# Two feed-forward blocks with their down projections computed by seven products a pair of chunks

## The chip, the cores and the metric

One core of one Trainium2 chip runs the whole kernel in one launch. The metric is the device time of one execution in microseconds (us). The kernel before took 758.54 us (median of 3 runs, 758.26 to 759.86). Two executions that differ by less than about 0.2% (1.5 us) can't be told apart here.

## The reference

The input is 256 tokens of width 1024. Two transformer blocks follow one another, each with one layer. What matters here are the two feed-forwards; around them lie projections, two kinds of attention and norms, which the change leaves as they are.

```
first block:   h = rms_norm(x, g);  x = x + (silu(h @ w_gate) * (h @ w_up)) @ w_down      # w_down is 2816 x 1024
second block:  h = rms_norm(x, g);  m = (relu(h @ w_up_2) ** 2) @ w_down_2                # w_down_2 is 4096 x 1024
               x = x + rms_norm(m, g_post)
```

Everything is in 32-bit floats. The kernel reaches that precision with a rounded 32-bit format on TensorE: a value v is split into `hi` (v rounded) and `lo` (v - hi, rounded), and each product a*b is the sum of three matmuls, hi*hi, hi*lo and lo*hi.

## The kernel before, in words

**Layout.** The 256 tokens are two tiles of 128 rows. Weights come in 232 "fills" of 128 x 1024 floats (512 KB): SyncE loads a fill into one of 4 raw buffers `w_raw`, ScalarE (ACT) rounds it into `w_hi` (`round_to`, line 1284), VectorE (DVE) subtracts to get `w_lo` (`cut_to`, line 1908), TensorE (PE) multiplies. Fill k can only be loaded when fill k - 4 has been cut. All programs are written out by hand, one in-order queue per engine, with semaphores between them; SyncE's queue of loads is in order too.

**Up projections** (`multiply_up`, line 888). The hidden vector is computed transposed: 128 hidden columns (a "chunk") by 256 tokens, 8 chunks of the contraction by 3 matmuls, each with 256 columns moving. In the first block two chunks of gate and two of up make one step (96 matmuls), 11 steps; in the second four chunks make a step (96 matmuls), 8 steps. A fill holds two of the 8 contraction chunks for the four outputs of a step.

**Down projections** (`multiply_down` through `chunk`, line 453; for the last step line 930). A chunk of the hidden vector times 128 rows of the down weight: 2 token tiles, 3 matmuls, 2 halves of 512 output columns, 12 matmuls of 512 columns a chunk. PSUM banks 4 to 7 keep the four quarters of the output (2 token tiles by 2 column halves) through the whole feed-forward; banks 0 to 3 take the up products. PE does the up part of step i and then the down part of step i - 1.

**Between up and down.** First block: DVE multiplies the gate by the row scale (`scale_gate`, line 2387), ACT applies SiLU (line 1613), DVE multiplies by up (`times_up`, line 2393), ACT rounds (line 1608), DVE cuts (line 2377). Second block: ACT applies ReLU (line 1870), GpSimd (POOL) squares (line 2955), ACT squares and rounds (line 1876), DVE cuts.

**Ends.** First block: `add_residual` (line 2371) adds each quarter, scaled by its row's norm, to x; PE then turns x (lines 582, 593), ACT and DVE split it (lines 1302, 1928), and the next projection starts (line 506). The last down step goes quarter by quarter, so three of the four additions run beside matmuls. Second block: ACT squares each quarter with a row sum (line 1703), DVE scales (line 2553), POOL takes the inverse root (line 2785), DVE adds to x (line 2567), SyncE and ACT store.

Of the kernel before, what the change touches and what calls it, by code (L numbers as in the profile page):

```python
# [10 lines left out]
F32R = mybir.dt.float32r  # L11
# [4 lines left out]
P = 128  # L16
D = 1024
# [22 lines left out]
D_FF2 = 4 * D  # L40
MASKED = -1e30
# [52 lines left out]

def laid_out(inputs):
# [17 lines left out]
    arrays["rope1m"] = np.ascontiguousarray(rope[SEQ:])  # L113
    return arrays
# [5 lines left out]
class Weights:  # L120
# [5 lines left out]
    def __init__(self, a):  # L126
# [11 lines left out]
        n = D_FF // 11  # L138
        for i in range(12):
            if i < 11:  # L140
                self.first["up1", i] = len(self.fills)
                for s in range(4):
                    pieces = []
                    for w, name in enumerate(("w_gate", "w_up")):
                        rows = a[name][0][2 * s * P:(2 * s + 2) * P, i * n:(i + 1) * n].rearrange("(c p) n -> p c n", p=P)
                        pieces.append((lambda raw, w=w: raw.rearrange("p (c w n) -> p c w n", c=2, w=2)[:, :, w, :], rows))
                    self.fills.append(pieces)
            if i > 0:
                self.slab(("down1", i - 1), a["w_down"][0][2 * (i - 1) * P:2 * i * P, :], 2, D)
# [15 lines left out]
        for i in range(9):  # L165
            if i < 8:
                self.slab(("up2", i), a["w_up_2"][0][:, i * WIDE:(i + 1) * WIDE], KC, WIDE)
            if i > 0:
                self.slab(("down2", i - 1), a["w_down_2"][0][4 * (i - 1) * P:4 * i * P, :], 4, D)
# [28 lines left out]
    def used(self, name):  # L198

        last = self.first[name] + {"qb": 4, "kb": 4, "vb": 4, "kva": 2, "qa": 4}.get(name, 4)  # L200
        return last if name[0] != "down1" else last - 2
# [18 lines left out]
spread_done spread_copied gate_scaled acted hidden_done hidden_rounded hidden_cut  # L220
# [6 lines left out]
Semaphores = namedtuple("Semaphores", SEMAPHORES + ["w_landed", "x_landed", "turned_landed", "post_landed", "stored"])  # L227


def program(nc, a, out):  # L230
    with ExitStack() as ctx:
# [6 lines left out]
                       stored=[sems[f"stored{t}"] for t in range(TILES)], **sems)  # L238
# [9 lines left out]
def allocate(nc, ctx, T):  # L248
# [67 lines left out]
    T.ffn_rows = sb("ffn_rows", [P, TILES, WIDE])  # L316
    T.f_hi = sb("ffn_hi", [P, 4, SEQ], F32R)
    T.f_lo = sb("ffn_lo", [P, 4, SEQ], F32R)
# [4 lines left out]
    T.pT2 = sb("pT2", [P, 2, NG + 1, P])  # L323
    T.wspT = sb("w_spatial_T", [P, TILES, TILES, GROUPS, P])
    T.bsp = sb("b_spatial", [P, TILES, GROUPS])
    T.qk = {c: sb(f"{c}2_rows", [P, TILES, WIDE]) for c in "qk"}
# [13 lines left out]
    T.spread = T.u_rows[:, 0, 0:SEQ]  # L340
    T.hid_hi, T.hid_lo = (T.f_hi, T.q2T["q"]), (T.f_lo, T.q2T["k"])
# [35 lines left out]
BANKS = {"qb": 0, "kb": 1, "vb": 3, "oa": 5, "ob": 8, "down1": 11, "b": 14, "o1": 17, "down2": 18}  # L377
FFN1_STEPS, FFN2_STEPS = 11, 8
# [7 lines left out]
def squared(place, t, half):  # L386

    return 2 * t + half + 1 if place == 0 else 4 + 2 * half + t + 1
# [5 lines left out]


def up_banks(i):

    return (4, 5, 6, 7) if i == 0 else (0, 1, 2, 3)
# [12 lines left out]
def sync_program(nc, a, out, T, S, W):  # L411
    sp = nc.sync
    rows_out = rows_of(out)
    sp.dma_start(T.w_raw[:, 0:1, 0:WIDE], W.half).then_inc(S.half_landed, 16)
    for k, pieces in enumerate(W.fills):
# [13 lines left out]
        for view, src in pieces:  # L429
            sp.dma_start(view(T.w_raw[:, r, :]), src).then_inc(S.w_landed[r], 16)  # L430
    for t in range(TILES):
# [8 lines left out]
def tensor_program(nc, T, S, W):  # L440
    pe, bank, ident = nc.tensor, T.bank, T.ident

    def w(half, k, c, per):
        n = SLOT // per
        return half[:, k % SLOTS, c * n:(c + 1) * n]
# [424 lines left out]
    def feed_forward(up, down, steps, chunks, ready, taken, cut0, cut_per, spread, rounded, right=None):  # L870
        def multiply_down(i, first):
            for c in range(chunks):
                k = W.first[down, i] + c
                pe.wait_ge(*W.cut(S, k))
                if c % 2 == 0:
                    pe.wait_ge(S.hidden_cut, cut0 + i * cut_per + c // 2 + 1)
                mm = chunk(T.hid_hi[i % 2], T.hid_lo[i % 2], k, 0, 1, c, ((4, 5), (6, 7)), WIDE, first and c == 0, False)
                mm.then_inc(S.w_used, 1)

        def multiply_up(i, s, c, passes):  # L880

            k, kc = W.first[up, i] + s, 2 * s + c
            w_hi, w_lo = w(T.w_hi, k, c, 2), w(T.w_lo, k, c, 2)
            for b in range(4):
                cols, outs = slice(b * P, (b + 1) * P), bank[up_banks(i)[b]][:, 0:SEQ]
                for n, (x, y) in enumerate(((w_hi, T.h_hi), (w_hi, T.h_lo), (w_lo, T.h_hi))):
                    if n in passes:
                        mm = pe.matmul(outs, x[:, cols], y[:, kc, :], start=kc == 0 and n == 0,  # L888
                                       stop=kc == KC - 1 and n == (1 if i == 0 else 2))
            return mm  # L890
# [2087 lines left out]
```

## Time and profile before

| | |
|---|---|
| median of 3 runs | 758.54 us |
| profiled execution, its own time | 758.59 us |
| span of the profiled execution, first to last instruction | 757.3 us |
| PE busy | 98% of the span |
| DVE busy | 60% |
| ACT busy | 49% |
| GpSimd busy | 15% |
| granted TensorE clock, mean | 0.999 |
| matmuls | 4394 |
| HBM read | 128.6 MB, 171 GB/s over the span |

The span is 1.3 us shorter than the execution's own time; the difference is what lies before the first and behind the last instruction. The feed-forward of the first block lies from 130.8 to 322.5 us of the span, that of the second from 570.0 to the end. Busy times count an instruction from its start to its end; matmuls overlap, so the cost of one is read from the distance between starts.

### The profile page before, as it was taken

The page shows a single profiled execution, that of the slowest core. Times are in us where ns is not written, and L with a number is a line of the kernel's source. Part 1 is how long each engine was busy: PE and PEld are TensorE (multiplying, and loading weights), DVE is VectorE, ACT ScalarE, POOL GpSimd, SP SyncE. Part 2 cuts the span into 40 slices and gives each one's busy share as a digit, 9 for nine tenths or more (in the row PEclk, how much of TensorE's full clock was granted, in tenths as well). Part 3 has the DMA queues.
Part 4 walks back from the last instruction along what each step waited for, and adds up shares of the span by engine and source line. Part 5 has one row for each costly group of instructions (what it writes and reads, how often), then busy time and mean ns, then how long its engine had stood idle before and what let it go on. Part 6 is the DMA issues. An engine that isn't in the chain of part 4 may idle for free.

```text
span 757.3 us, 11043 instructions
## 1 busy us (share of the span) xinstructions
PE 739.8 (98%) x4394; PEld 641.1 (85%) x4394; DVE 457.8 (60%) x635; ACT 373.3 (49%) x535; POOL 112.5 (15%) x138
## 2 busy tenths in 40 slices
PE   6999999999999999999999999999999999999996
PEld 5877778999999999888888888888779899998895
DVE  5898695766555555465747555674948754455433
ACT  6666754644444434285443534664338644444431
POOL 2867550100000000001110000000302111001110
PEclk9999999999999999999999999999999999999999
DMA  9642142787665666446536543474535766656511
GB/s 318 207 132 82 58 160 92 229 284 220 189 212 172 195 216 208 133 142 219 169 110 195 194 139 112 123 250 147 178 107 198 260 192 187 206 184 191 180 46 56
DMA packets 70179, 130.46 MB, mean 172 GB/s; under 512 B 5312, under 2 KB 29072, under 8 KB 70128
## 3 DMA queue, kind: packets, MB, share of 16 engines
q1 hardware_dynamic: 68144, 125.00, 52.3%
q0 software_dynamic: 1552, 4.20, 1.7%
q8 instruction: 35, 0.57, 0.3%
q10 hardware_dynamic: 432, 0.56, 0.2%
q14 instruction: 16, 0.13, 0.0%
HBM read 128.62 MB, written 1.05 MB: 171 GB/s over the span
## 4 chain that ended last, share of the span: by engine, by line
PE 93%; DVE 3%; DMA 2%; issue 1%; ACT 1%; SPq 0%; DVEq 0%; ACTq 0%
PE psum L453 41%; PE psum L888 29%; PE psum L506 12%; PE psum L930 2%; DMA w_raw<-in_w_in 2%; PE psum L680 1%; PE psum L601 1%; PE psum L546 1%; PE psum L631 1%; PE psum L1058 1%; PE psum L582 1%; PE psum L652 1%; DVE b_ratio L2154 0%; PE psum L992 0%; PE psum L1020 0%
## 5 line engine op out<-in xcount | busy, mean ns | idle before, releaser
L1908 DVE TENSOR_TENSOR w_lo<-w_raw,w_hi 128x1024 fp32r<-128x1024 f32 x225 | 275.2, 1235 | 158.3 <-ACT w_hi L1284 157.7
L1284 ACT ACTIVATE w_hi<-w_raw 128x1024 fp32r<-128x1024 f32 x231 | 241.2, 1059 | 180.7 <-PE psum L888 78.6
L888 PE MATMUL psum<-h_hi,w_hi 128*128 128x256 f32 x608 | 170.3, 284 | 0.6 <-issue 0.6
L888 PE MATMUL psum<-h_hi,w_lo 128*128 128x256 f32 x608 | 169.5, 283 | 0.0
L888 PE MATMUL psum<-h_lo,w_hi 128*128 128x256 f32 x608 | 161.8, 281 | 0.0
L888 PEld LDWEIGHTS psum<-h_hi,w_hi 128*128 128x128 f32 x608 | 114.7, 189 | 1.7 <-issue 0.7
L888 PEld LDWEIGHTS psum<-h_hi,w_lo 128*128 128x128 f32 x608 | 114.4, 188 | 0.0
L888 PEld LDWEIGHTS psum<-h_lo,w_hi 128*128 128x128 f32 x608 | 111.1, 189 | 0.7
L453 PE MATMUL psum<-w_hi,h_hi 128*128 128x512 f32 (+1 forms) x240 | 94.5, 394 | 0.0
L453 PE MATMUL psum<-w_hi,h_lo 128*128 128x512 f32 (+1 forms) x240 | 93.0, 387 | 0.0
L453 PE MATMUL psum<-w_lo,h_hi 128*128 128x512 f32 (+1 forms) x240 | 92.9, 387 | 0.0
L453 PEld LDWEIGHTS psum<-w_hi,h_lo 128*128 128x128 f32 x240 | 45.1, 188 | 10.1
L453 PEld LDWEIGHTS psum<-w_lo,h_hi 128*128 128x128 f32 x240 | 45.2, 188 | 9.3
L453 PEld LDWEIGHTS psum<-w_hi,h_hi 128*128 128x128 f32 x240 | 45.1, 188 | 9.2
L506 PE MATMUL psum<-w_hi,h_hi 128*128 128x512 f32 x128 | 52.6, 411 | 0.0
L506 PE MATMUL psum<-w_lo,h_hi 128*128 128x512 f32 x128 | 50.4, 394 | 0.0
L506 PE MATMUL psum<-w_hi,h_lo 128*128 128x512 f32 x128 | 46.6, 395 | 0.0
L453 PE MATMUL psum<-w_hi,ffn_hi 128*128 128x512 f32 x120 | 37.9, 397 | 0.0
L453 PE MATMUL psum<-w_lo,ffn_hi 128*128 128x512 f32 x120 | 37.7, 395 | 0.0
L453 PE MATMUL psum<-w_hi,ffn_lo 128*128 128x512 f32 x120 | 37.6, 394 | 0.0
L2955 POOL TENSOR_TENSOR u_rows<-ffn_rows 128x512 f32<-128x512 f32 x16 | 16.9, 1075 | 135.2 <-ACT ffn_rows L1870 135.2
L506 PEld LDWEIGHTS psum<-w_hi,h_hi 128*128 128x128 f32 x128 | 24.1, 188 | 6.3 <-issue 0.6
(303 smaller groups left out, 992.7 us busy)
## 6 DMA issues: line engine op xcount, KB each, us to landing
w_raw<-in_w_in SPq DMA_DIRECT2D x77, 512.0 KB, 4.5
w_raw<-in_w_down SPq DMA_DIRECT2D x54, 512.0 KB, 4.3
w_raw<-in_w_up SPq DMA_DIRECT2D x32, 512.0 KB, 4.4
w_raw<-in_w_gate SPq DMA_DIRECT2D x44, 256.0 KB, 2.9
w_raw<-in_w_up SPq DMA_DIRECT2D x44, 256.0 KB, 3.4
w_raw<-in_w_out SPq DMA_DIRECT2D x16, 512.0 KB, 4.0
w_raw<-in_w_branch_a SPq DMA_DIRECT2D x4, 512.0 KB, 4.6
w_raw<-in_w_branch_b SPq DMA_DIRECT2D x4, 512.0 KB, 4.6
```

The costliest lines, as they stand in the source:

```text
L453: mm = pe.matmul(bank[b][:, 0:width], x[:, kc, t * P:(t + 1) * P], y[:, h * width:(h + 1) * width], start=first and n == 0, stop=last and ...
L506: mm = pe.matmul(out, x[:, kc, t * P:(t + 1) * P], y, start=n == 0 and i == 0, stop=last and i == 2)
L546: mm = pe.matmul(bank[7][0:32 + META, :], T.meta_stack[:, kc, :], y, start=kc == 0 and n == 0, stop=kc == KC - 1 and n == 1)
L582: tr = pe.transpose(bank[b][:, j * SEQ + t * P:j * SEQ + (t + 1) * P], src[:, t, c * P:(c + 1) * P], ident[:])
L601: tr = pe.transpose(bank[b][:, c * SEQ + t * P:c * SEQ + (t + 1) * P], src[:, t, (2 * n + c) * P:(2 * n + c + 1) * P], ident[:])
L631: mm = pe.matmul(bank[b][:, 0:KEYS], x[rows, c, t * P:(t + 1) * P], y[rows, c // 2 if kind == "a" else c, :], start=i == 0, stop=i == 2)
L652: tr = pe.transpose(bank[MAP_BANK][:, c * SEQ + t * P:c * SEQ + (t + 1) * P], T.maps[:, t, h if kind == "a" else 2 * h, c * P:(c + 1) * P] ...
L888: mm = pe.matmul(outs, x[:, cols], y[:, kc, :], start=kc == 0 and n == 0, stop=kc == KC - 1 and n == (1 if i == 0 else 2))
L930: mm = pe.matmul(bank[4 + 2 * t + h][:], x[last][:, c, t * P:(t + 1) * P], y[:, s, cols], start=False, stop=c == chunks - 1 and n == 2)
L1284: act.activation(T.w_hi[:, k % SLOTS, :], T.w_raw[:, k % RAW_SLOTS, :], ACT.Copy).then_inc(S.w_rounded, 1)
L1908: dve.tensor_tensor(T.w_lo[:, k % SLOTS, :], T.w_raw[:, k % RAW_SLOTS, :], T.w_hi[:, k % SLOTS, :], ALU.subtract).then_inc(S.w_cut, 1)
L2955: pool.tensor_tensor(T.u_rows[:, j, :], rows, rows, ALU.mult).then_inc(S.hidden_done, 1)
```

## The change

The two down projections are computed with the Strassen-Winograd scheme. A pair of chunks of the hidden vector (2 x 128 columns) and the two halves of the output make a 2 x 2 block product: A (tokens by hidden, quarters A11, A12, A21, A22) times B (hidden by output). Instead of 8 products of quarters, 7 products of sums of quarters are accumulated, over all pairs but the last of a feed-forward, in seven PSUM banks (0 to 6). After the last such pair the output quarters are formed from the seven sums once. The last pair is done in the plain way, quarter by quarter (8 products). So a pair costs 21 matmuls of 512 columns instead of 24: 10 of 11 pairs in the first block, 15 of 16 in the second.

What else moves with it:

- The four quarters of a pair's down weight are loaded from a new layout into `pair_raw` (three quarters) and, twice, into `pair_t` (the fourth): 768 KB + 512 KB a pair instead of 1 MB. DVE forms four sums of quarters (`add_pair`, `sum_pair`, `sum_pair_rest`); ACT rounds all seven (`round_pair`, three instructions of 1536, 1024 and 1024 columns), DVE cuts all seven (`cut_pair`, the same sizes). Before, two fills of 1024 were rounded and cut.
- DVE forms four sums of the hidden quarters (`sum_hidden`, `_2`, `_3`: 256, 128 and 128 columns); ACT rounds and DVE cuts seven quarters (896 columns) a pair; before four (512).
- The up weights come in a new layout, one fill for all 8 contraction chunks of 128 hidden columns. The first group of a feed-forward needs two fills at once (`up_first`), which were one before. Up fills go round 4 slots instead of 8, the other 4 slots hold every second pair's seven quarters.
- Up products of chunk after chunk all go into bank 7 (`up_two`). ACT copies them out (`take_up`; in the second block `take_hidden` with ReLU) before the next may start. `scale_gate` and `times_up` work on chunks from SBUF (256 columns) instead of two chunks from PSUM (512).
- The squares of the second block are done by ACT alone (`square_hidden`), not by GpSimd and ACT.
- At the end of each feed-forward DVE forms three intermediate sums and the quarters from the product banks; in the first block GpSimd takes two of the additions (`add_x`).
- SyncE's queue has a pair load behind every second or fourth up fill; a pair load waits until the pair two before it has been cut.

```diff
-    def feed_forward(up, down, steps, chunks, ready, taken, cut0, cut_per, spread, rounded, right=None):
+PRODUCT = {1: (1, 0, 2), 2: (3, 2, 0), 3: (7, 1, 1), 4: (2, 6, 6), 5: (5, 3, 5), 6: (6, 5, 3), 7: (4, 4, 4)}
+EARLY, LATE, LAST = (1, 2, 3), (7, 5, 6, 4), (1, 6, 7, 4, 5, 2, 3)
...
+    def down(q, products, first=False, last=False):
+        buf, i = pair_place(q)
+        pe.wait_ge(S.hidden_cut, q + 1)
+        for n_product, p in enumerate(products):
+            x, y, b = PRODUCT[p]
+            pe.wait_ge(S.pair_cut, pair_parts(q) + NEEDS[p])
...
+            for n, (u, v) in enumerate(((x_hi, y_hi), (x_hi, y_lo), (x_lo, y_hi))):
+                mm = pe.matmul(bank[b][:], u, v, start=first and n == 0, stop=last and n == 2)
...
+    for i in range(2, PAIRS1):                      # PE, first block
...
+        down(i - 2, EARLY, first=i == 2)
+        chunk_up1(2 * i)
...
+        down(i - 2, LATE, first=i == 2)
+        chunk_up1(2 * i + 1)
+    down(LAST1 - 1, LAST, last=True)
+    pe.wait_ge(S.up_taken, 2 * PAIRS1)
+    down_quarters(1)
...
+    for i in range(2, PAIRS2):                      # PE, second block
+        if i > 2:
+            pe.wait_ge(S.up_taken, 2 * PAIRS1 + i)
+            up_two(W.first["up2", 2 * i], 7)
...
+        down(FIRST2 + i - 2, EARLY, first=i == 2)
...
+        down(FIRST2 + i - 2, LATE, first=i == 2)
+    down(LAST2 - 1, LAST, last=True)
+    pe.wait_ge(S.up_taken, 2 * PAIRS1 + PAIRS2)
+    down_quarters(2)
...
+        if i < PAIRS2:                              # DVE, second block, iteration i, q = FIRST2 + i - 1
+            add_pair(q)
+            cut_pair(q, 0)
+            sum_pair(q)
+            sum_hidden(q, 2 * PAIRS1 + i)
+            sum_pair_rest(q)
+            sum_hidden_2(q)
+            cut_pair(q, 1)
+            sum_hidden_3(q)
+            cut_pair(q, 2)
+            cut_to(min(f + 2 * i + 6, len(W.fills)))
...
+        cut_hidden(q)
...
+            for part in range(3):                   # ACT, second block, iteration i
+                round_pair(q, part)
+            take_hidden(i)
+            round_to(min(f + 2 * i + 6, len(W.fills)))
+            square_hidden(i)
...
+        round_hidden(q)
...
+    for i in range(1, PAIRS1):                      # DVE, first block
+        sum_hidden(i - 1, 2 * i)
+        add_pair(i - 1)
+        cut_pair(i - 1, 0)
+        sum_hidden_2(i - 1)
+        scale_gate(2 * i)
+        sum_hidden_3(i - 1)
+        cut_fill(f + 4 * i + 4)
+        sum_pair(i - 1)
+        times_up(2 * i)
+        sum_pair_rest(i - 1)
+        cut_fill(f + 4 * i + 5)
+        cut_hidden(i - 1)
+        cut_pair(i - 1, 1)
+        cut_pair(i - 1, 2)
...
+        scale_gate(2 * i + 1)
+        cut_fill(f + 4 * i + 6)
+        times_up(2 * i + 1)
+        cut_fill(f + 4 * i + 7)
```

## Rows read from the trace of the kernel before

**Rows 1.** The page, part 1: busy us, share, instructions.

```profile
PE 739.8 (98%) x4394; PEld 641.1 (85%) x4394; DVE 457.8 (60%) x635; ACT 373.3 (49%) x535; POOL 112.5 (15%) x138
```

**Rows 2.** The page, part 4: the chain that ended last, by engine.

```profile
PE 93%; DVE 3%; DMA 2%; issue 1%; ACT 1%; SPq 0%; DVEq 0%; ACTq 0%
```

**Rows 3.** Windows of one step of each block: length, busy us by engine, clock, DMA.

```profile
207.85:224.98 17.13, 17.13 (x121) 16.03 (x120) 9.33 (x9) 7.41 (x9) 0.55 (x1) 1.00 0.65 207
615.92:638.64 22.72, 22.72 (x145) 20.53 (x144) 10.92 (x10) 10.38 (x12) 2.04 (x2) 1.00 0.62 187
```

**Rows 4.** The chain in order of time, second block: start, us, work.

```profile
604.49 11.39 PE psum L888 x96
615.88 11.21 PE psum L453 x48
627.09 11.52 PE psum L888 x96
```

**Rows 5.** Groups of VectorE instructions by form: busy us, mean ns.

```profile
L2377 DVE TENSOR_TENSOR k2T<-u_rows,q2T 128x512 fp32r<-128x512 f32 x8 | 5.1, 684 | 0.0
L2371 DVE SCALAR_TENSOR_TENSOR x<-psum,row_scale,x 128x512 f32<-128x512 f32 x4 | 3.0, 750 | 4.8 <-PE psum L930 4.8
```

**Rows 6.** VectorE in order of time: start, us (of a merged run), count.

```profile
137.08 4.63 DVE L1908 TENSOR_TENSOR w_lo<-w_raw,w_hi 128x1024 fp32r<-128x1024 f32 x4
157.35 1.23 DVE L1908 TENSOR_TENSOR w_lo<-w_raw,w_hi 128x1024 fp32r<-128x1024 f32 x1 [1.26 <-ACT w_hi L1284]
734.63 0.15 DVE L2756 SCALAR_TENSOR_TENSOR stat<-row_scale 128x2 f32<-128x2 f32 x1
734.82 0.16 DVE L2758 TENSOR_TENSOR row_scale<-row_scale 128x2 f32<-128x2 f32 x1
```

**Rows 7.** ScalarE in order of time.

```profile
145.45 3.89 ACT L1284 ACTIVATE w_hi<-w_raw 128x1024 fp32r<-128x1024 f32 x4
156.26 1.06 ACT L1284 ACTIVATE w_hi<-w_raw 128x1024 fp32r<-128x1024 f32 x1 [1.42 <-DMA w_raw<-in_w_down]
582.95 1.15 ACT L1876 ACTIVATE ffn_hi<-ffn_rows 128x512 fp32r<-128x512 f32 x2
```

**Rows 8.** In order of time, where the first feed-forward starts: VectorE, TensorE.

```profile
133.52 1.22 DVE L1908 TENSOR_TENSOR w_lo<-w_raw,w_hi 128x1024 fp32r<-128x1024 f32 x1
144.26 0.36 PE L888 MATMUL psum<-h_hi,w_hi 128*128 128x256 f32 x1 [0.56 <-issue]
```

**Rows 9.** In order of time, end of the first feed-forward.

```profile
320.58 0.39 PE L930 MATMUL psum<-w_hi,ffn_lo 128*128 128x512 f32 x1
320.81 1.91 PE L582 MATMUL psum<-small,x 128*128 128x128 f32 x16
322.48 0.47 PE L506 MATMUL psum<-w_hi,h_hi 128*128 128x512 f32 x1
```

**Rows 10.** VectorE's cuts of the hidden vector, 575 to 600 us: ns min/median/max.

```profile
L2377 DVE TENSOR_TENSOR ffn_lo<-u_rows,ffn_hi x2: 678/1096/1514, 583.7 to 585.2; 128x512 fp32r<-128x512 f32 x2
```

**Rows 11.** In order of time, start of the second feed-forward: TensorE, VectorE, SyncE.

```profile
570.03 0.36 PE L888 MATMUL psum<-h_hi,w_hi 128*128 128x256 f32 x1
571.86 2.35 DVE L1908 TENSOR_TENSOR w_lo<-w_raw,w_hi 128x1024 fp32r<-128x1024 f32 x2
574.24 2.29 SPq L430 DMA_DIRECT2D w_raw<-in_w_up  x2
```

**Rows 12.** Transfers from 580 to 600 us.

```profile
DMA packets 2022, 5.55 MB, mean 278 GB/s; under 512 B 161, under 2 KB 161, under 8 KB 2019
w_raw<-in_w_up SPq DMA_DIRECT2D x4, 512.0 KB, 5.1
```

**Rows 13.** In order of time, the end of the kernel.

```profile
751.10 0.40 PE L930 MATMUL psum<-w_hi,k2T 128*128 128x512 f32 x1
753.32 1.41 DVE L2567 SCALAR_TENSOR_TENSOR x<-tmp,stat,x 128x512 f32<-128x512 f32 x2
754.76 0.65 ACTq L1887 DMA_DIRECT2D out<-x  x1
```

More of the change, by code:

```diff
@@ L40 @@
 D_FF2 = 4 * D
+PAIRS1, PAIRS2 = D_FF // (2 * P), D_FF2 // (2 * P)
 MASKED = -1e30
@@ L137, in __init__ @@
             self.slab((name, 0), a["w_out"][0][h * WIDE:(h + 1) * WIDE, :], 4, D)
[L138 to L149, printed above, removed]
+        for f in range(2 * PAIRS1):
+            self.first["up1", f] = len(self.fills)
+            for w in range(2):
+                self.fills.append([(lambda raw: raw, a["up1"][f, :, w, :])])
         win2 = a["w_in_2"][0]
@@ L198, in used @@
     def used(self, name):
[L200 to L201 removed]
+        return self.first[name] + {"kva": 2}.get(name, 4)
 SEMAPHORES = """
@@ new lines, in scalar_program @@
+    f = W.first["up2", 0]
+    round_to(f + 8)
+    round_pair(FIRST2, 0)
+    take_hidden(0)
+    take_hidden(1)
+    square_hidden(0)
+    square_hidden(1)
+    for i in range(2, PAIRS2 + 1):
+        q = FIRST2 + i - 1
+        if i == 2:
+            round_pair(FIRST2, 1)
+            round_pair(FIRST2, 2)
+            round_hidden(FIRST2)
+        if i < PAIRS2:
[4 more added lines that the diff above has]
+            square_hidden(i)
+        else:
+            for part in range(2):
+                round_quarters(q, part)
+        round_hidden(q)
@@ L1886, in scalar_program @@
+    copy_first(2)
+    for n, (t, half) in enumerate(((0, 0), (0, 1), (1, 0), (1, 1))):
+        square_last(n, t, half, T.last[t, half])
     act.wait_ge(S.x_posted, 8)
@@ L2395, in vector_program @@
-    f = W.first["up1", 0]
-    for i in range(FFN1_STEPS):
-        last = i == FFN1_STEPS - 1
-        cut_to(f + 8 if i == 0 else f + 6 * i + 9)
-        scale_gate(i)
-        times_up(i)
-        cut_to(f + 9 if i == 0 else f + 6 * i + 10)
-        if not last:
-            cut_to(f + 10 if i == 0 else f + 6 * i + 11)
-        cut_hidden(i, i, 0, T.ffn_rows[:, i % 2, :].rearrange("p (c n) -> p c n", c=2))
-        if not last:
-            cut_to(f + 6 * i + 12)
-    last = W.first["z", 1]
@@ L2416, in vector_program @@
+    dve.wait_ge(S.product_done, 7)
+    dve.wait_ge(S.x_part, 2)
+    step(add_x(bank[1][:], 1, 1))
+    for n, (t, half, b) in enumerate(QUARTER_BANKS[1]):
+        dve.wait_ge(S.quarter_done, n + 1)
+        own()
+        add_x(bank[b][:], t, half).then_inc(S.x_added, 1)
+    cut_pairs("h3", (0, 1), (5, 6), gain(2), T.h_hi, T.h_lo)
+    cut_pairs("h3", (2, 3), (2, 3), gain(2), T.h_hi, T.h_lo)
     r3 = [T.row_scale[:, 2, t:t + 1] for t in range(TILES)]
@@ L2765, in vector_program @@
     post_add(1, 0, HALVES)
+    scale_last(2)
+    end_last(3)
+    scale_last(3)
     post_mean(1, 1)
-    post_scale(1, 1, 1, 7, T.bg[1], scale[1])
     post_add(1, 1, HALVES)
```

631 lines of the change are left out of this document (435 added, 196 removed).

## The prediction

> **What bounds the kernel now.** Read the page's first part, then the chain of waits, then windows. TensorE is busy 98% of the span [rows 1] and holds 93% of the chain that ended last [rows 2]; DVE (60%) and ACT (49%) have room, on average. One step of either feed-forward shows it stage by stage: 17.13 us and 22.72 us in which TensorE never pauses, while DVE works 9.33 and 10.92 us and ACT 7.41 and 10.38 us [rows 3]. So the reader should expect that fewer matmuls shorten the time, until DVE or ACT, which pay for it, come up to TensorE. The chain in order of time gives the price of a matmul: 96 up matmuls take 11.39 and 11.52 us, so 0.119 us each, and 48 down matmuls 11.21 us, so 0.233 us each [rows 4].
>
> **What goes.** The first block loses 10 x 3 = 30 matmuls of 512 columns, 7.0 us, the second 15 x 3 = 45, 10.5 us. The up matmuls are as many as before. That is the whole gain: 17.5 us if TensorE never waits. Beside it the 0.56 us in which TensorE stood after the first step [rows 8] goes: the wait for the spread scale now stands two chunks later.
>
> **DVE's price.** A cut of 512 columns takes 0.684 us [rows 5], one of 1024 columns 1.23 us [rows 6]: 1.06 ns a column and 0.14 us. But four of 1024 in a row take 4.63 us [rows 6], so they start 1.13 us apart: 1.06 ns a column and only 0.05 us. Where an instruction waits for the one just before it, it starts 0.04 us after that one's end (734.63 + 0.15, then 734.82 [rows 6]), some 0.13 us more. ACT's run of four takes 3.89 us [rows 7], 0.95 us apart; two of 512 columns take 1.15 us, 0.5 us apart [rows 7].
>
> *First block, a pair.* TensorE: 21 x 0.233 + 96 x 0.119 = 16.35 us (17.13 before). DVE: 18 instructions, 12160 columns: 12160 x 1.06 ns + 18 x 0.05 = 13.8 us, with few waits on itself, because another instruction stands between. ACT: 11 instructions, 8448 columns, some 8 us. I laid out one pair from the end of an up chunk (0): ACT takes bank 7 by 0.65, before the 9 EARLY matmuls end at 2.1, so the next chunk isn't held; `cut_hidden` ends at 14.4, where TensorE wants it at 16.35. Steady state: bound by TensorE. Cost 0; if DVE needed 19% more, this cover would be gone.
>
> *Second block, a pair.* TensorE: 21 x 0.233 + 48 x 0.119 = 10.6 us (11.36 before). DVE: 12 instructions, 9088 columns: 9.6 + 0.6 = 10.2 us, and two waits on itself (`sum_pair`, `sum_pair_rest`), 10.45. One iteration: `sum_pair_rest` ends at 4.7; ACT then rounds part 2, takes the chunks, rounds two fills, squares and rounds the hidden quarters: 0.95 + 0.5 + 1.9 + 0.5 + 0.94 = 4.8, so 9.55; DVE's last cut starts at 9.6 and ends its iteration at 10.6. Three engines with the same period: no spare anywhere. I take 10.6 for each, so steady state costs nothing, but a late start is never made good.
>
> **The starts and ends.** These eat the gain.
>
> *Start of the first block.* The second group of `up_first` needs the fill whose cut ends at 133.52 + 1.22 [rows 8]: +0.3. The first pair's hidden sums are ready late, since no down matmuls stretch the first four chunks. Chunk 2 ends near 149.9; DVE is through with chunk 1, the pair's sum and first cut only at 152.1, and needs 5.4 more until `cut_hidden` ends at 157.5; TensorE is there at 155.6: +1.9.
>
> *End of the first block.* In the pair before the last, `cut_quarters` (1.67 + 0.6) puts DVE behind: `scale_gate(21)` at 2.4 after the last up chunk, not 0.7; with two fills and the last `times_up` in between, the last hidden cut ends at 6.05, where the 21 LAST matmuls end at 4.9: +1.15. Then DVE has 12 instructions of 512 columns (0.6 to 0.7 each, four of them waiting on the one before) and waits for GpSimd's second addition, before the four quarters can be added. By my count the last addition ends 15.3 after the last up chunk, TensorE at 11.7. Before, the last matmul and the next projection's first lay 320.58 + 0.23 to 322.48 apart, transposes included: 1.7 us [rows 9]. Now 4.4: +2.7. GpSimd beside a two-input DVE instruction can cost more: one cut beside a square took 1514 ns, another 678 [rows 10]; bound 0 to +1.7 for two such, I take 0.
>
> First block: -7.0 - 0.55 + 0.3 + 1.9 + 1.15 + 2.7 = **-1.5 us**.
>
> *Start of the second block.* `up_first` asks for two fills at once. The first of the two DVE cuts that start at 571.86 is the second fill; it ends at 573.1, where TensorE starts at 570.03 now [rows 11]: +3.1, nothing else can run. Then pair 0: before, the two up fills issued at 574.24 [rows 11] landed in 5.1 us [rows 12]. Now 1.28 MB of pair load stand ahead of them in SyncE's queue; at the 278 GB/s that this stretch reached [rows 12] that is 4.6 us, at most. `round_pair` and `add_pair` of pair 0 stand behind both fills on ACT and DVE, so pair 0 is ready near 594.1 and TensorE, with three chunk pairs done, at 590.5: +3.6 (bounds 0.4, the load hidden, and 4.6). Next, `take_hidden(2)` stands behind all of pair 1's rounding: up pair 3 needs bank 7 at 4.9, ACT is done at 6.3: +1.4. The fill behind two pair loads lands 1.2 late, once: +1.2 (0 to 2).
>
> *End of the second block.* The last two whole pairs have no fills (8.9 us for DVE), but TensorE, 1.4 late in phase, still waits +1.0 for pair 14. After that the quarters: DVE's forms, `end_last`, `scale_last`, mean, root, `post_add` run as 17 instructions of 512 columns from 22 us after the hidden cut of pair 12, to 36.7; the last matmul ends at 28.4. So 8.3 + 2.55 for the store; before, the last matmul (751.4) to DVE's last (754.73) is 3.3 [rows 13] and the store the same 2.55. +5.0 (3 to 7).
>
> Second block: -10.5 + 3.1 + 3.6 + 1.4 + 1.2 + 1.0 + 5.0 = **+4.8 us**.
>
> SiLU, gelu and the masks' loads on GpSimd have slack of tens of us; 0. GpSimd's squares gone: 0, they were off the chain, and DVE has no GpSimd beside it in steady state. The squares of x3 stand ahead of two fills of ACT; the fills are wanted 11 us after the projection starts and are there at 6: 0.
>
> **A rule of the skill.** DVE's row says 1.13 us from start to start of 1024 columns where one alone takes 1.23 [rows 6]. The Trainium skill, "VectorE: DVE Perf Modes", section on the trn2 errata, gives a 32-bit two-input instruction (N + 151)/0.96 ns and says many small instructions pay the fixed part each time; its section "The DRAIN you can't avoid" says the next does not start until the pipe is empty, except where it isn't held. By the full rule a pair of the second block would take DVE 9088/0.96 + 12 x 157 ns = 11.35 us; by the exception the 10.2 above. The trace's runs side with the exception.
>
> **Sum.** In the profiled execution's own frame: 758.59 - 1.5 + 4.8 = **761.9 us**; the median of the runs, 758.54, is the same within 0.1.
>
> **Rivals.**
>
> *DVE unhidden (slower still).* If 512- and 128-column instructions with semaphores don't overlap like the runs of 1024, each costs its full 0.14 us and the waits: 9088 x 1.06 + 12 x 0.14 = 11.3 us a pair. For: a DVE that waits for ACT at each step never starts early. Against: the order puts other work between. Twelve pairs with fills at +0.7 to +0.9: +8 to +11, so 771 us.
>
> *Transfers bind (slower).* A pair of the second block moves 2.3 MB in 10.6 us, 222 GB/s, issued in one burst behind the last cut of the pair before. 278 GB/s were reached over 20 us [rows 12]; if bursts with the doubled quarter only reach 200, a pair takes 11.8: +13, 775 us.
>
> *Faster: the waits at the starts aren't there.* The mechanism: SyncE's loads overtake, so that the two fills land in 5.1 us despite the pair load ahead, pair 0 is ready with TensorE (0.4 instead of 3.6), DVE then runs ahead of TensorE by more than the 1.4 of phase, and those 1.4, 1.2 and 1.0 vanish too. -6.8: 755.1 us. It decides from DVE's iteration taking under 10.3 us: then lateness is made good over 12 pairs. For it: transfers share 16 engines and don't queue strictly. Against: ACT's chain of 9.55.
>
> *No change.* Only half of that: the fills land in time, the rest stays, 758.7 us.
>
> **Chances.** Forecast 0.50; DVE unhidden 0.12; transfers bind 0.08; faster 0.15; no change 0.15. A measurement of this kernel tells 0.2%, 1.5 us. So faster 0.15, same 0.15, slower 0.70. The range: below, it reaches to the faster case but not past it, 756; above, to the lower part of the DVE case, 769. Outside lie some 0.2.
>
> **What would show it.** The windows of one step: 16.4 us in the first block and 10.6 us a pair in the second, DVE busy over 95% in the latter. TensorE idle before the first up group of the second block near 3 us, and before its first down matmul 3 to 4 us. After the last matmul 10 to 11 us to the end of the span. If a pair of the second block takes 11.3 or more, DVE's overlap is the failed step; if TensorE doesn't wait for the first pairs, the landing times are. Wrong altogether would be a first block that isn't at 16.4 a pair.

## The result, and the profile after

The changed kernel took 774.08 us (median of 4 runs, 772.60 to 775.98), the kernel before 758.71 in the same session: a ratio of 1.0202, 95% interval 1.0176 to 1.0227. The direction was right, the size was not: 761.9 was forecast and 756 to 769 the range. The profiled execution is the slowest of the four, 775.98 us, 1.9 above the median; its span is 774.7 us.

The page of the kernel after, part 1, the engines of part 4 and one row of part 6, which answer to [rows 1, 2, 12]:

```profile
PE 732.0 (94%) x4319; PEld 631.0 (81%) x4319; DVE 598.0 (77%) x852; ACT 433.2 (56%) x611; POOL 101.8 (13%) x126
...
PE 69%; DVE 16%; DMA 8%; issue 4%; ACT 2%; POOL 1%; SPq 0%; ACTq 0%; DVEq 0%
...
w_raw<-in_up SPq DMA_DIRECT2D x76, 512.0 KB, 5.1
```

There are 75 matmuls fewer, as meant. The chain tells the rest: TensorE held 93% of it and now holds 69%; DVE and the transfers of up fills took the difference. Part 6 hides the latter, because its median is over all fills. So the next view is the chain in order of time, where the second block starts and behind (start, us, work; kernel after):

```profile
578.45 9.77 DMA w_raw<-in_up
588.29 1.07 ACT w_hi L1429
...
599.12 1.04 DVE hidden_lo L2654
...
623.34 9.00 DMA w_raw<-in_up
...
655.24 10.38 DMA w_raw<-in_up
...
677.96 10.73 DMA w_raw<-in_up
...
701.04 9.54 DMA w_raw<-in_up
```

From 578 us to 711 us the chain goes through DVE and, in about every second pair, through an up fill that takes 9 to 11 us from its issue to its landing, where [rows 12] had 5.1.

**Steady pairs.** Windows of the kernel after, as [rows 3] (length, busy us by engine PE, PEld, DVE, ACT, POOL, clock, DMA share, GB/s): one pair of the first block, two of the second, and a longer stretch of the second.

```profile
209.00:225.40 16.40, 16.40 (x121) 15.46 (x120) 14.44 (x19) 9.72 (x12) 0.55 (x1) 1.00 0.72 231
645.44:668.16 22.72, 22.72 (x151) 20.42 (x151) 21.39 (x25) 14.84 (x17) 0.00 (x0) 1.00 0.65 218
650.50:692.70 42.20, 40.72 (x267) 36.48 (x267) 39.09 (x45) 28.50 (x31) 0.00 (x0) 1.00 0.61 207
```

The first block's pair is 16.4 us, as forecast (16.35). In the second block TensorE would do four pairs of 10.55 in the 42.2 us of the third row, and it stands for 1.5 of them. The starts of `hidden_lo` (`cut_hidden`), one a pair, give the period: 599.07, 612.85, 623.41, 634.88, 645.44, 656.29, 668.16, 678.72, 691.24, 701.80, 713.12, 723.89, 734.45. The first period is 13.8 us; of the eleven behind it five are 10.56 us and six lie between 10.8 and 12.5. These eleven take 121.6 us, where 11 x 10.55 is 116.05.

**Where the time lies.** Starts of the first matmul of each stage, profiled executions:

| stage | before | after | longer | forecast |
|---|---|---|---|---|
| start to first up matmul | 130.79 | 131.77 | +0.98 | 0 |
| first feed-forward, to the next projection's first matmul | 191.69 | 194.42 | +2.73 | -1.5 |
| from there to the second feed-forward's first matmul | 247.55 | 250.97 | +3.42 | +3.1 |
| second feed-forward, to the end of the span | 187.27 | 197.54 | +10.27 | +1.7 |
| span | 757.3 | 774.7 | +17.4 | +3.3 |

(The forecast's +4.8 for the second block contains the 3.1 of the third line.) Two lines hold the miss: 4.2 us in the first feed-forward, 8.6 in the second. The +0.98 of the first line isn't the change's: the kernels of experiments 1 to 4 have the same instructions up to there and start at 130.30 to 130.54.

TensorE's waits, kernel after: before the first down matmul of the first block, its second instruction (at half the clock: the third starts at 160.81, 0.43 us behind it, where [rows 4] had 0.233), before the last pair's quarters, the transposes; second block: first up matmul, first down matmul, the down's second half.

```profile
159.82 0.76 PE L1024 MATMUL psum<-pair_hi,hidden_hi 128*128 128x512 f32 x1 [3.39 <-issue]
160.38 0.63 PE L1024 MATMUL psum<-pair_lo,hidden_hi 128*128 128x512 f32 x1
...
315.16 0.47 PE L1044 MATMUL psum<-pair_hi,hidden_hi 128*128 128x512 f32 x1 [1.43 <-issue]
...
323.80 2.63 PE L684 MATMUL psum<-small,x 128*128 128x128 f32 x16 [2.93 <-DVE x L2715]
...
577.16 0.55 PE L978 MATMUL psum<-h_hi,w_hi 128*128 128x256 f32 x1 [2.98 <-ACT h_hi L1444]
...
600.26 0.76 PE L1024 MATMUL psum<-pair_hi,hidden_hi 128*128 128x512 f32 x1 [3.64 <-issue]
...
606.38 0.80 PE L1024 MATMUL psum<-pair_hi,hidden_hi 128*128 128x512 f32 x1 [1.95 <-ACT up_rows L2073]
...
763.48 0.40 PE L1044 MATMUL psum<-w_hi,hidden_lo 128*128 128x512 f32 x1
```

The releaser of the fifth row is misnamed, as can happen with a wait for several: the first quarter of `h_hi`, which is all that this matmul needs of it, was there before 574.3; what ended at 577.07 is DVE's cut of the second fill. Experiment 1 moves that cut alone, and the wait is gone. Windows behind three of these waits, kernel after (granted clock is the third from the end):

```profile
159.82:164.00 4.18, 4.18 (x10) 3.31 (x11) 4.18 (x6) 2.09 (x4) 0.00 (x0) 0.50 0.57 211
577.16:582.22 5.06, 5.06 (x24) 5.06 (x25) 5.06 (x9) 3.25 (x4) 1.17 (x1) 0.53 0.69 194
600.26:609.40 9.14, 7.19 (x16) 5.20 (x17) 7.10 (x9) 3.02 (x5) 0.00 (x0) 0.51 0.79 275
```

Before, the clock was 1.00 at these places. A granted clock of 0.50 is the lower level, 1.2 GHz: after each of these three stretches without work TensorE ran at half speed, for about 5.7, 4.8 and 9.0 us, the last with the wait of 1.95 us in it. After the 2.93 us before the transposes it did not: there the clock is 1.00 (313.7 to 327 us). In the profiled executions of experiments 1, 2 and 4, which have the same instructions there, it did fall (0.65, 0.62 and 0.76 over the transposes). So the lower clock doesn't follow each such wait. How much of the time it is, experiments 4 to 6 measure.

### The profile page after: what moved, and what is told of

Same layout as the page of the kernel before. It is cut to its first block, busy times and chain, and to the rows that moved or that the text cites. A ratio compares the mean times of both kernels' runs of the same rounds, so it can differ in the third digit from the quotient of the medians.

```text
span 774.7 us, 11228 instructions
## 1 busy us (share of the span) xinstructions
PE 732.0 (94%) x4319; PEld 631.0 (81%) x4319; DVE 598.0 (77%) x852; ACT 433.2 (56%) x611; POOL 101.8 (13%) x126
## 4 chain that ended last, share of the span: by engine, by line
PE 69%; DVE 16%; DMA 8%; issue 4%; ACT 2%; POOL 1%; SPq 0%; ACTq 0%; DVEq 0%
PE psum L555 22%; PE psum L978 17%; PE psum L608 12%; PE psum L1024 8%; DMA w_raw<-in_up 6%; DVE w_lo L2138 3%; DVE w_lo L2603 2%; DMA w_raw<-in_w_in 2%; DVE pair_lo L2603 2%; PE psum L782 1%; DVE pair_sums L2616 1%; DVE hidden_lo L2654 1%; PE psum L703 1%; PE psum L648 1%; PE psum L733 1%
## 5 line engine op out<-in xcount | busy, mean ns | idle before, releaser
L2138 DVE TENSOR_TENSOR w_lo<-w_raw,w_hi 128x1024 fp32r<-128x1024 f32 x171 | 209.5, 1239 | 48.3 <-ACT w_hi L1429 47.8
L1429 ACT ACTIVATE w_hi<-w_raw 128x1024 fp32r<-128x1024 f32 x177 | 184.1, 1058 | 61.3 <-DMA w_raw<-in_w_in 36.0
L978 PE MATMUL psum<-h_lo,w_hi 128*128 128x256 f32 x608 | 164.2, 283 | 0.0
L978 PEld LDWEIGHTS psum<-h_hi,w_hi 128*128 128x128 f32 x608 | 116.0, 191 | 10.2 <-ACT up_rows L2073 5.5
L978 PEld LDWEIGHTS psum<-h_hi,w_lo 128*128 128x128 f32 x608 | 116.0, 191 | 0.0
L555 PEld LDWEIGHTS psum<-w_hi,h_hi 128*128 128x128 f32 x240 | 45.1, 188 | 9.2
L1801 ACT ACTIVATE up_rows<-psum 128x512 f32<-128x512 f32 x22 | 13.1, 597 | 65.5 <-PE psum L978 65.5
L1024 PE MATMUL psum<-pair_hi,hidden_hi 128*128 128x512 f32 x91 | 38.3, 420 | 9.9 <-issue 7.0
L1768 ACT ACTIVATE pair_hi<-pair_raw 128x1536 fp32r<-128x1536 f32 (+1 forms) x26 | 32.9, 1265 | 18.3 <-DVE pair_raw L2629 18.3
L1768 ACT ACTIVATE w_hi<-tmp 128x1536 fp32r<-128x1536 f32 (+1 forms) x24 | 30.4, 1265 | 16.8 <-DVE tmp L2629 16.8
L2603 DVE TENSOR_TENSOR pair_lo<-pair_raw,pair_hi 128x1536 fp32r<-128x1536 f32 (+1 forms) x26 | 38.6, 1486 | 0.0
```

The source lines that it names most:

```text
L555: mm = pe.matmul(bank[b][:, 0:width], x[:, kc, t * P:(t + 1) * P], y[:, h * width:(h + 1) * width], start=first and n == 0, stop=last and ...
L978: mm = pe.matmul(out, x, y[:, kc, :], start=kc == 0 and n == 0, stop=kc == KC - 1 and n == last_pass)
L1024: mm = pe.matmul(bank[b][:], u, v, start=first and n == 0, stop=last and n == 2)
L1429: act.activation(T.w_hi[:, W.slot[k], :], T.w_raw[:, k % RAW_SLOTS, :], ACT.Copy).then_inc(S.w_rounded, 1)
L1768: act.activation(T.pair_hi[buf][:, places, :], src, ACT.Copy).then_inc(S.pair_rounded, 1)
L1801: act.activation(T.rows[:, j % 2, :].rearrange("p (c n) -> p c n", c=2), src, ACT.Copy).then_inc(S.up_taken, 1)
```

## The experiments

Theory at the start: the 12 us that my sum missed are not in the steady pairs' work but in three starts: (a) waits at the beginning of each block, (b) the half clock behind them, (c) pair loads ahead of up fills in SyncE's queue. The rival: the scheme as such is too expensive for DVE, whatever the order.

**1. The second up fill earlier.** DVE cuts it before the input's halves.

```diff
+    cut_fill(W.first["up2", 0] + 1)
     post_out(1)
     add_out2(1)
     cut_h4(0)
     cut_h4(1)
-    cut_fill(W.first["up2", 0] + 1)
     cut_fill(W.first["up2", 0] + 2)
```

> The changed kernel (774.1 us), with VectorE's cut of the second up fill of the second block moved ahead of the post-norm of the second token tile, into a stretch where VectorE has 1.5 us to spare. The theory that a wait of TensorE costs its length and a stretch at the lower granted clock (0.50 from 574.5 to 581.3 us): the 2.98 us wait before the first up matmul of the second block goes, and with it most of the low-clock stretch (some 2 us): 769 us. The rival, the clock doesn't depend on this wait: 771 us, with the stretch still there. A second rival, pair 0 is late by as much more on VectorE: no gain, 774.

Measured 772.25 us, ratio 1.0171 (1.0154 to 1.0187), nearer to the rival's 771 than to 769. The wait went (first up matmul at 572.88, without a pause) and a part came back at the next fills, and with it the lower clock (0.50 from 578.6 to 581.0 us; kernel with the second fill early):

```profile
578.63 0.55 PE L978 MATMUL psum<-h_hi,w_hi 128*128 128x256 f32 x1 [2.40 <-DVE w_lo L2138]
```

It gained 1.8 of 3.1 us: the third and fourth fill, behind the input's halves on ACT and DVE, are late next.

**2. The up fills ahead of the pair loads** in SyncE's queue.

```diff
-        if j2 % 2 == 1 and j2 > 2:
-            load_pair(FIRST2 + (j2 - 3) // 2)
+        if j2 == 3:
+            load_pair(FIRST2)
+        if j2 % 2 == 1 and j2 > 6:
+            load_pair(FIRST2 + (j2 - 5) // 2)
+    load_pair(LAST2 - 1)
     load_pair(LAST2)
```

> The changed kernel with only SyncE's queue of the second block in another order: each pair load (from the second on) is issued behind the next two up fills, not ahead of them. Same bytes. The theory that the up fills are late because they stand behind a pair load that itself waits for a cut: the 3.6 us wait before the first down matmul of the second block shrinks to under 1 us, the 2.8 us wait of the next pair goes, the steady pair falls from 11.2 to 10.6 us; 774 - 3 - 3 - 6 - low clock 3 = 760 us. The rival, that bytes bind (2.3 MB a pair) whatever the order: pair loads are late instead, 771 to 774 us.

Measured 768.52 us, ratio 1.0125 (1.0110 to 1.0140): 5.6 us under the changed kernel, with not a byte fewer. Its chain from 602 to 700 us holds TensorE alone, 4.8 and 5.7 us in turn, and no transfer. The same window in the kernel with the fills first, and one of its waits:

```profile
650.50:692.70 42.20, 42.20 (x279) 38.64 (x279) 41.92 (x49) 29.43 (x33) 0.00 (x0) 1.00 0.68 225
```
```profile
602.55 0.79 PE L1027 MATMUL psum<-pair_hi,hidden_hi 128*128 128x512 f32 x1 [3.81 <-ACT up_rows L2076]
```

TensorE never stands, and DVE is busy for 41.9 of 42.2 us. So the 10.55 us a pair were there to be had; SyncE's order prevented it. The second row is the wait that I had at 1.4 us: `take_hidden(2)` behind pair 1's rounding. Of the expected 760 the wait before the first down matmul came true (0.66 us) and so did the steady pairs; this wait grew from 1.95 to 3.81 instead of going, and the lower clock stayed (0.91 on average from 600 to 640 us).

The transfers themselves didn't become faster. Issues from 574 to 625 us, with their median time to landing, kernel after and kernel with the fills first:

```profile
w_raw<-in_up SPq DMA_DIRECT2D x9, 512.0 KB, 9.0
```
```profile
w_raw<-in_up SPq DMA_DIRECT2D x11, 512.0 KB, 9.0
```

In both kernels two fills are issued right behind a pair load and take 9 us. With the fills first they are those that are wanted one pair later, so the 9 us are covered. The rival, that bytes bind, falls: this kernel moves 225 GB/s in the window above, the changed kernel 207.

**3. Both.** 

> Both earlier repairs together: the second up fill of the second block is cut before the input's halves, and the two up fills of the fourth chunk pair are loaded ahead of the pair loads. If what each saved alone adds up (1.8 and 5.6 us under 774.1), 766.7. If both only free the same late start of the first pair of the second block (the chain from the landing of the seventh and eighth up fill to the first down matmul), it is no better than the fills first alone: 768.5.

Measured 765.96 us, ratio 1.0091 (1.0076 to 1.0106). 8.1 us together, 7.4 as a sum: they add up.

**4. TensorE kept busy in four waits** by matmuls whose result is overwritten; the output stays the same.

```diff
+    def keep_busy(b, n):
+        for _ in range(n):
+            pe.matmul(bank[b][:], T.h_hi[:, 0, 0:P], T.h_hi[:, 0:2, :], start=True, stop=True)
...
         if i == 2:
             pe.wait_ge(S.spread_copied, 1)
+            keep_busy(2, 14)
         down(i - 2, EARLY, first=i == 2)
```

> The changed kernel with extra matmuls on TensorE (results thrown away, the bank is started anew behind them) in the four long waits: 14 before the first down matmul of the first block, 12 before the first up matmul of the second, 15 before its first down matmul, 12 before that pair's second half. No wait is shortened. If the low-clock stretches (23.9 us at half clock in all) come from TensorE standing still and cost time, the granted clock stays at 1.00 and the time falls by 5 to 9 us, to 767. If the low clock costs nothing because TensorE waits for others there anyway, 774. If the extra matmuls are late and push the real ones, 775 or more.

Measured 774.27 us, ratio 1.0200 (1.0184 to 1.0216): no gain at all, though the clock stayed up in all four places. Window and chain, kernel kept busy:

```profile
158.50:162.70 4.20, 4.20 (x27) 3.82 (x28) 4.20 (x6) 2.12 (x4) 0.00 (x0) 1.00 0.73 257
```
```profile
575.39 9.42 DMA w_raw<-in_up
...
597.15 9.90 DMA w_raw<-in_up
...
619.39 9.77 DMA w_raw<-in_up
...
641.49 9.99 DMA w_raw<-in_up
```

In the first block, where TensorE is the bound, the clock gave 1.6 to 2.2 us: 130.44 to 322.70 is 192.26 us, against 194.42 in the changed kernel and 193.9 to 194.0 in experiments 1 to 3, whose first block is the same. In the second it gave nothing, since there the chain lies on fills and DVE, not on TensorE: from the first up matmul to the first `hidden_lo` 21.56 us against 21.91, the first period 13.93 against 13.78. The stage took 199.8 instead of 197.5 us. The 2.3 lie in the eleven periods behind, 124.1 us instead of 121.6: every second pair waits for a fill again, now 1.0 to 2.3 us. Why the fills came still later is open. My theory (b) falls for the second block.

**5. The same wait in the kernel before.** Its first up matmul of the second block waits for the second fill's cut.

```diff
-                pe.wait_ge(*W.cut(S, k))
+                pe.wait_ge(*W.cut(S, k + 1 if up == "up2" and i == 0 and s == 0 else k))
```

> The kernel before with one wait more: the first up group of the second block also waits for the cut of the second fill, 3.1 us later, as in the changed kernel. Nothing else. If a wait costs its own length only: 758.7 + 3.1 = 761.8. If it also brings a low-clock stretch of 6.8 us, as in the changed kernel, up to 2.5 us more: 764.

Measured 763.56 us, ratio 1.0062 (1.0047 to 1.0077): 4.8 us, which leaves 1.7 beside the 3.1 of wait, in a kernel where nothing covers either. The traces say 1.5: from the first up matmul of the block to the end 188.74 us against 187.27. The lower clock lies right behind the wait (first row this kernel, second the kernel before, same length):

```profile
572.50:580.00 7.50, 6.14 (x37) 6.14 (x38) 7.49 (x11) 5.04 (x8) 1.61 (x1) 0.65 0.64 208
```
```profile
570.00:577.50 7.50, 7.48 (x62) 7.28 (x61) 7.21 (x13) 6.07 (x12) 0.43 (x1) 1.00 0.41 131
```

**6. Only the first block's start reordered.** TensorE does the fifth up chunk, in a free bank, before the first down matmuls; ACT loads SiLU's table before it is needed; DVE cuts that chunk's second fill earlier.

```diff
+            up_two(W.first["up1", 4], 6)
             pe.wait_ge(S.spread_copied, 1)
-        down(i - 2, EARLY, first=i == 2)
-        chunk_up1(2 * i)
+            down(0, EARLY, first=True)
...
+    act.activation(T.stat[:, 1:2], T.stat[:, 0:1], ACT.Silu)
     take_up(0)
```

> Only the start of the first block is reordered in the changed kernel (fifth up chunk before the first down matmuls, SiLU table early). Theory A: the wait of 3.4 us and the half clock behind it are the whole surprise of this start; TensorE then has no wait there and the first block takes 188.7 us as in the kernel with both starts, not 194.4; all of it reaches the end: 768.3. Rival: what TensorE gains here VectorE doesn't follow, and a wait of 2 us or more comes up in the next pair: 771 or more.

Measured 769.34 us, ratio 1.0141 (1.0124 to 1.0158): 4.7 us, 1.0 less than theory A had. The stage took 319.67 - 130.64 = 189.03 us, 5.4 less than after, with no wait of TensorE between 140 and 175 us. Less the wait of 3.39 that leaves 2.0, or 1.5 against the 193.9 us of experiments 1 to 3; I put it down to the clock, which is 1.00 from 140 to 175 us here. The edit changes three things at once, so what SiLU's table alone is worth isn't shown.

**7. Both blocks' starts reordered.** Experiments 3 and 6 together, and in the second block: DVE and ACT do pair 0's quarters before the seventh and eighth fill; TensorE does the fourth chunk pair before the first down matmuls; ACT takes the third chunk pair before it rounds pair 1; `up_first` goes fill pair by fill pair, and DVE cuts the last halves of the input ahead of the third and fourth fill.

```diff
-    cut_to(f + 8)
+    cut_to(f + 6)
     add_pair(FIRST2)
     cut_pair(FIRST2, 0)
     sum_pair(FIRST2)
-    sum_hidden(FIRST2, 2 * PAIRS1 + 1)
+    cut_pair(FIRST2, 1)
     sum_pair_rest(FIRST2)
...
+    cut_to(f + 8)
+    sum_hidden(FIRST2, 2 * PAIRS1 + 1)
```

> Both starts reordered: in the first block TensorE does the fifth up chunk (bank 6) before the first down matmuls, the SiLU table is loaded early; in the second block the pair's weights are summed and cut before the seventh and eighth up fill, TensorE does the fourth chunk pair before the first down matmuls, its bank is emptied before pair 1 is rounded, and up_first goes fill pair by fill pair. Theory A (late starts and the half clock behind them are what my sum missed, and VectorE's pace of 10.5 us a pair then sets the end): the first block loses its 3.4 us wait and 2.8 us of half clock (-5.5), the second gains 2.4 over the fills first alone, as VectorE starts so much earlier: 760. Theory B (TensorE's own work sets the end of the second block): 5.5 + 10 under 768.5, so 753. Theory C (the waits only move on): 766 or more.

Measured 755.64 us, ratio 0.9955 (0.9940 to 0.9970): 18.4 us less than the changed kernel, and faster than the kernel before by 3.5. Theory A had 760 and B 753; the truth lies between them. The stages: 188.73 us (before 191.69), 248.89 (247.55), 186.97 (187.27). In the second block the chain is DVE's until 600 us, and `hidden_lo` then starts every 10.55 us for twelve pairs on end (588.47, 599.02, 609.56, ... 715.05). In the changed kernel the same twelve took 135.4 us, here 126.6: 8.8 of the 10.6 us that this block gains. In this stretch TensorE is as full as DVE (650.50 to 692.70: 42.20 and 41.93 us of 42.20), so which of the two holds the other can't be told.

**8. The first block's end reordered too.** The last pair's quarters are cut between `scale_gate` and `times_up`, and two fills of the next projection behind the hidden cut.

> The same, and at the end of the first block the cuts of the next projection's first two fills and of the last pair's quarters are moved out of VectorE's way: the last hidden cut comes 1.4 us earlier, before TensorE wants it, and one cut of 1.2 us less stands ahead of the four quarters. If VectorE's order at this end is what made it 1.5 us worse than I had counted: 2.6 us under the kernel with the two starts, so near 757. If GpSimd's additions set it: no more than 0.5 us under it.

Measured 755.64 us, ratio 0.9951 (0.9934 to 0.9967): nothing. The transposes start earlier but run slower (first row this kernel, second the kernel with both starts; the granted clock over them is 0.50 in the first and 0.73 in the second):

```profile
315.35 3.68 PE L687 MATMUL psum<-small,x 128*128 128x128 f32 x16 [3.70 <-DVE x L2740]
```
```profile
316.71 3.18 PE L687 MATMUL psum<-small,x 128*128 128x128 f32 x16 [2.94 <-DVE x L2734]
```

Of the 1.36 us, 0.54 were there before the feed-forward began (130.27 against 130.81, where the kernels don't differ). Of the other 0.82, 0.5 went in the transposes, at the lower clock, and 0.5 in what follows up to the second block, so nothing is left.

**9. The sum that GpSimd waits for, earlier**, on top of 8.

> The kernel with both starts and the first block's end reordered, and there the sum that GpSimd waits for (the fourth intermediate) is formed before the first output quarter. Theory A: GpSimd's second addition starts right behind its first, 1.2 us earlier, VectorE's wait of 1.0 us for it goes, the transposes start 1.0 us earlier: 754.6. Rival (this end is covered by what the lower clock behind the idle stretch takes back): 755.6.

Measured 755.34 us, ratio 0.9956 (0.9942 to 0.9971): the rival's number, by another mechanism. The transposes start no earlier (315.33, in experiment 8 315.35). DVE's wait for GpSimd is gone, but GpSimd's work now lies beside other instructions of DVE, which became slower (kernel with the early sum):

```profile
307.67 2.08 DVE L2158 TENSOR_TENSOR w_lo<-w_raw,w_hi 128x1024 fp32r<-128x1024 f32 x1
...
311.84 1.25 DVE L2740 SCALAR_TENSOR_TENSOR x<-pair_raw,row_scale,x 128x512 f32<-128x512 f32 x1
```

2.08 for 1.22 and 1.25 for 0.75: 1.36 us lost. Won are the wait of 1.01 and 0.31 of an addition that took 1.06 in experiment 8 and takes 0.75 here: the same. By this the two additions cost DVE about what they would if it did them itself, 2 x 0.75; no run has DVE do them.

**10. The fourth quarter loaded once**, from the third pair on of either block (the output isn't the reference's).

> The fourth quarter of a pair is loaded once, not twice, from the third pair on of either block: 1.0 MB a pair, the output is not the reference's. Theory A (the order in SyncE's queue is at fault: the up fills stand behind a pair load): the pair load is a fifth shorter, so the fills come some 1 us earlier in the pairs in which TensorE waits for them: -1 to -2, 772 to 773; TensorE still waits for fills in every second pair. Rival (bytes: transfers bind at the doubled quarter): the waits for fills vanish and it gains what the changed order gained, 5.6 us: 768.5.

Measured 770.22 us, ratio 1.0154 (1.0138 to 1.0169): -3.9 us, between the two theories. On its chain two transfers of an up fill are left, and none from 605 us on:

```profile
576.75 10.67 DMA w_raw<-in_up
599.20 5.61 DMA w_raw<-in_up
```

So order and bytes are one thing: what counts is whether a fill, with the pair load ahead of it, lands before it is wanted. Experiment 2 has it issued a pair earlier, this one shortens what stands ahead. Ahead of the seventh and eighth fill the load is still double, and there nothing is gained (first up matmul to first down matmul 24.0 us, in the changed kernel 23.1).

**11. Four of the seven sums at the end left out**, on top of 7 (the output isn't the reference's).

> The kernel with both starts, without four of VectorE's seven sums of products at the end of the second block (the output is not the reference's). Theory A (VectorE's instructions behind the last matmuls are the tail's price): 4 x 0.67 = 2.7 us less than 755.6: 753.0, the tail 8.5 instead of 11.2 us. Rival (squares on ScalarE and the mean set the tail): within 0.7 of 755.6.

Measured 754.05 us (753.21 to 754.74), 1.6 less by the medians. In the traces the last hidden cut is 17.8 us from the end with the sums (737.61, span 755.4) and 15.2 without (737.59, span 752.8): 2.6, which is DVE's 4 x 0.67. The medians say less: the profiled execution of the kernel with the sums is 1.0 above its median, that of the other is at it. That the tail is DVE's is shown by the traces, its price to within 1 us.

**12. Pair 1's hidden quarters ahead of two fills**, on top of 9.

> The kernel with the early sum, and at the start of the second block the hidden quarters of pair 1 are rounded and cut ahead of the ninth and tenth up fill, not behind them. Theory A (from 570 to 600 us VectorE's chain sets the time, and from then on VectorE and TensorE go at the same 10.55 us a pair, so what is gained at the start arrives whole at the end): TensorE's second down starts 2.3 us earlier, VectorE's next pair 0 to 2 us earlier: 1 to 2 us less than 755.3, 753.3 to 754.3. Rival (VectorE has the same work in another order, its pace alone counts): 755.3, and TensorE waits for the following pair what it no longer waits for this one.

Measured 756.14 us (11 runs, 755.11 to 758.07), ratio 0.9972 (0.9963 to 0.9981): no gain, the rival, and with the second half of it: before its second down matmuls TensorE waits 1.35 us instead of 3.57, and at 604.78 it waits 3.27 for ACT's `take_hidden`, where it did not before. `hidden_lo` of pair 1 starts at 595.20 instead of 597.67, that of pair 2 at 608.02 instead of 608.21, and the stage takes 186.95 us where it took 186.8. So where DVE and TensorE both go at their full pace of 10.55 us a pair, this order didn't matter.

## Why the prediction was wrong

**What goes, 17.5 us.** Right: 75 matmuls fewer, 0.233 us each, pairs of 16.4 us in the first block.

**DVE's price.** Right, and with it the case of an unhidden DVE falls: a pair takes DVE 10.48 us (experiment 2), 10.45 was laid out. By the Trainium skill, "VectorE: DVE Perf Modes", trn2 errata, with its fixed part in full each time, an estimate from its figure is 11.35 us; the exception that its section "The DRAIN you can't avoid" allows is what the trace has, four pairs in 42.2 us. "Three engines with the same period: no spare anywhere" was right for TensorE and DVE, 42.20 and 41.92 us of 42.20. ACT was busy for 29.4 of them; it has gaps, in which it waits for DVE. My count of ACT in the first block was too low, without effect: I had 11 instructions, 8448 columns and 8 us a pair; it is 12 instructions of 10112 columns, and the window has 9.72 us.

**The failed step: steady state of the second block at no cost.** I wrote that it "costs nothing, but a late start is never made good", and charged one late fill, "1.2 late, once". It is not once. A pair's two up fills are issued right behind the 1.28 MB of a pair load, which is itself released by the last cut of the pair before; so the fills land 9 to 11 us after their issue, and they are wanted within a period of 10.55. ACT's rounding, DVE's cut and the next load follow from that landing. Six of the eleven periods behind the first were 0.2 to 2 us too long, the first five of them for a fill: 5.5 us together, where I had 1.2. Experiment 2 turns the order and gets 5.6 us, experiment 10 shortens the load and gets 3.9. I had reasoned about this queue for pair 0 and looked at all others by a mean rate only, 222 GB/s against 278. A mean rate doesn't see that the fills stand last in each burst. My rival "Transfers bind" names that burst, and its 775 us is near what was measured; but its mechanism, a rate too low for the bytes, is not what happened: experiment 2 moves the same bytes at 10.55 us a pair.

**Second block, the other terms.** The wait for the second fill, +3.1: right (577.16 for 574.1; experiment 5 has it alone). Pair 0, +3.6: the wait was 3.64, but by luck. From the first up matmul to the first down matmul I had 21.0 us (573.1 to 594.1), and it took 23.10: behind the landing of its fill, ACT and DVE needed 12 us, not 10.2. TensorE came 2.1 us later than I had it too, at the lower clock, so the difference of the two stayed the same. `take_hidden(2)`, +1.4: 1.95, and 3.81 once the fills come early; with half clock behind it the first period took 13.8 us, where I had 12.0 (10.6 and 1.4). Pair 14, +1.0: 0.60. The tail, +5.0: right to the tenth (763.48 to 774.7 is 11.2, before 6.2). Of the 8.6 us by which this block missed, 2.1 are thus pair 0, 1.8 the first period and 4.3 the fills in the periods behind it.

**First block, -1.5 forecast, +2.7 measured.** The first pair's wait was 3.39, not 1.9: SiLU's table load, 1.28 us, stands ahead of the first `silu`. The trace of before has it too, while ACT waited anyway, and I passed over it (first row before, second after):

```profile
140.03 1.28 ACT L1613 ACT_TABLE_LOAD   x1
```
```profile
146.65 1.28 ACT L1805 ACT_TABLE_LOAD   x1
```

Behind the wait came the half clock, 1.5 to 2.2 us by experiments 4 and 6, which my sum lacked altogether. At the end, TensorE waited 1.43 for the last hidden cut (1.15 forecast) and 2.93 before the transposes; from the last matmul to the next projection's first it took 5.5 us, 4.4 was forecast. The bound of +1.7 for GpSimd beside DVE, which I took as 0, was real: DVE's addition took 1.21 instead of 0.75, and it waited 1.01 for GpSimd.

**The half clock** was in none of my terms, though they made TensorE idle for 3 us in several places. Alone it costs 1.5 to 2.2 us an occasion where TensorE is the bound (experiments 4, 5, 6), and nothing where another engine sets the pace (experiment 4, second block).

**The faster case** was not a case of this kernel but of its order: "SyncE's loads overtake" didn't happen by itself, experiment 7 brought it about by hand. 755.1 was forecast for it, 755.64 measured; with the first block's start repaired too, and with another order, so the agreement is mostly luck.

What stays open: why the fills came later with TensorE kept busy, why the clock fell behind some waits of about 3 us and not behind others, and 1 us between medians and traces in experiment 11.

## What to carry to other kernels

When a change takes all slack out of an engine, price each start and each period's transfers, not the mean: lateness isn't made good. Here the starts and the order of the loads together were worth 18.4 us, the saving itself 17.5. For an in-order queue of loads ask what stands ahead of the transfer that is wanted next, in microseconds, in each period; a mean rate with room says nothing about it. A wait of 3 us that a change adds to a TensorE that never paused cost 1.5 to 2.2 us more of half clock here, and only where TensorE was the bound.

## What the runs showed of the hardware

Two-input DVE instructions of different sizes and sources, with semaphores satisfied, overlap as runs of equal ones do: twelve instructions and 9088 columns a pair in 10.48 us. A GpSimd addition of 512 columns beside DVE made DVE's instruction 0.31 to 0.86 us longer; in the largest case a GpSimd multiplication lay beside it too. A 512 KB fill issued right behind a 1.28 MB pair load landed 9 to 11 us after its issue, and in 9.0 us (median) in the kernel with the fills first, where that cost nothing. TensorE's granted clock was 0.50 behind waits of 2.40 to 3.81 us, for some 2 to 9 us; behind others of 2.65 (experiment 1), 2.93 (changed kernel), 2.96 (experiment 10) and 3.27 us (experiment 12) it stayed at 1.00.
